# Down-projection of a gated decoder block: block products over pairs of tiles in place of the plain product

## The chip, the cores and the metric

The kernel runs on one core of a Trainium2 chip. The metric is the device time of one execution in microseconds (us), the median of several runs. The core has a matrix engine (TensorE, PE), a vector engine (VectorE, DVE), an activation engine (ScalarE, ACT), a general engine (GpSimd, POOL), and SyncE (SP), whose queue issues nearly all DMA transfers here. Each engine runs its own instructions in order and waits for the others on semaphores. SBUF holds 128 partitions; PSUM has 8 banks of 128x512 float32 numbers, which matrix products accumulate in.

## The reference, cut to what matters

```
def gdfn(h, w_up, dw_w, dw_b, w_down):
    u = jnp.einsum("bsd,df->bsf", h, w_up)
    u = causal_dwconv(u, dw_w, dw_b)
    a, g = jnp.split(u, 2, axis=-1)
    return jnp.einsum("bsf,fd->bsd", jax.nn.gelu(a) * g, w_down)
...
    x = x + jnp.einsum("bsd,de->bse", merged, mix_w_out[l])
    h = rmsnorm(x, norm_ffn[l])
    x = x + gdfn(h, ffn_w_up[l], ffn_dw_w[l], ffn_dw_b[l], ffn_w_down[l])
return rmsnorm(x, norm_final)
```

There is one sequence of 1024 positions, D_MODEL is 1024 and D_FF is 2816. Before this part the layer has a convolution branch and a pooling branch, which the change leaves alone. All data are float32.

## The kernel before, in words

Channels lie on the partitions and positions along the row, so x is 8 tiles of 128x1024, and the gated activations gelu(a)*g are 22 tiles. For accuracy each float32 operand of a product is split in two parts: the high part is a rounded copy that ACT writes (w_high, gated_high), the low part is the operand less its high part, written by POOL for weights (w_low) and by DVE for gated tiles (gated_low). Each product of 128x128 by 128x512 is then three matmuls (three, lines 1395 to 1399): high by low, low by high, high by high.

The up-projection runs over pairs p = 0 to 21 of an a tile and a g tile. From pair 2 on it uses a seven-product scheme over a 2x2 blocking (output tile of the pair, half of the input channels) by (half of the input channels, half of the positions): seven products of 12 matmuls (PRODUCTS, in the order P1, P6, P5, P7, P2, P4, P3) take the place of eight. DVE does the sums after the products (lines 1294 to 1323), then the convolution's taps (line 1254), ACT the gelu (line 875), and DVE multiplies (gate, line 1269). The product, a gated tile, goes to DRAM (keep_g, line 428), since SBUF still holds h and its sums. The operands of the scheme lie in h_hi, h_lo, cv_r and ga_r; a part of these comes free with each product of the last pair, and becomes the home of gated tiles.

The down-projection follows. The 22 gated tiles are loaded back (load_g, line 434), one at a time in two buffers of tmp, split by ACT and DVE and put into 14 homes (G_HOME). The down weights are 44 operands of 128x512: for turn 0 to 3 (half of the gated tiles, half of the output tiles) 11 operands each. They come in 11 blocks of four (1 MB; ffn_weights, line 424) into two buffers, and pass through a ring of 8 places. PE does 4 output tiles by 2 halves for each operand (down_tile), accumulates over 11 gated tiles in PSUM, and DVE adds the result to x (evict, line 1340). The last turn runs half by half and quarter by quarter of the positions, and the final norm runs beside and behind it (lines 1356 to 1375).

SP issues in the order in which its program is written: around the up stage's end it stores the last gated tiles, loads the first ones, and then alternates a block, three gated tiles and a piece of x (lines 424 to 465). A load waits there until its buffer is free; a load written behind it is issued after it.

## Time and profile before

| what | value |
|---|---|
| median of 3 runs | 1348.48 us (1346.82 to 1350.67) |
| profiled execution | 1348.21 us, its span 1346.4 us, mean granted clock 0.996 |
| busy share of the span | PE 99%, DVE 58%, ACT 29%, POOL 54% |
| matmuls | 6084 |
| DMA | 118.65 MB, mean 88 GB/s |

The span reaches from the first to the last instruction, so the rest of the execution's time lies around it. Busy shares are means over stages with different limits. The up-projection's pairs fill the time up to about 1092 us, the down-projection and the final norm the rest.

### The profile page before, as it was taken

Reading aid. Unit: us, or ns where it says so; the run is one execution under the profiler, and the core shown is the slowest. Engines: PE = TensorE matmul, PEld = TensorE weight load, DVE = VectorE, ACT = ScalarE, POOL = GpSimd, SP = SyncE. Lnnn points to the kernel's source line nnn. Section 1 sums busy time; section 2 is a strip of 40 time slices with the busy share of each in tenths; the row PEclk is TensorE's granted clock in tenths of the full one; section 3 lists DMA queues with packets and bytes.
Section 4 is the critical chain, followed back from the end, with each engine's and each line's share of the span. In section 5 each row is a group of like instructions: output and inputs, shape, how many; then the busy total and the mean of one; then the engine's idle time right before and its main releaser. Section 6 shows DMA issues by size and latency. Waiting matters only on the chain.

```text
span 1346.4 us, 15879 instructions
## 1 busy us (share of the span) xinstructions
PE 1328.3 (99%) x6084; PEld 1106.2 (82%) x6084; DVE 783.8 (58%) x919; ACT 395.6 (29%) x534; POOL 721.8 (54%) x477
## 2 busy tenths in 40 slices
PE   8999999999999999999998999999999999999997
PEld 7888888888887888878887888888888888788887
DVE  5898999999556255536595545554455543320224
ACT  5212121211114440011154444444344433322210
POOL 4536645553553343366858978777787714424101
PEclk9999999999999999999999999999999999999999
DMA  9201111111111113244313212222222238431003
GB/s 336 79 32 53 41 47 48 33 59 34 47 47 48 47 48 109 78 172 134 117 43 114 94 63 94 91 82 68 90 94 78 94 133 304 173 110 63 0 1 125
DMA packets 33025, 118.65 MB, mean 88 GB/s; under 512 B 3136, under 2 KB 7232, under 8 KB 28864
## 3 DMA queue, kind: packets, MB, share of 16 engines
q1 hardware_dynamic: 29280, 108.31, 22.8%
q10 hardware_dynamic: 3680, 9.44, 1.9%
q8 instruction: 45, 0.74, 0.2%
q14 instruction: 20, 0.16, 0.0%
HBM read 97.82 MB, written 19.92 MB: 87 GB/s over the span
## 4 chain that ended last, share of the span: by engine, by line
PE 87%; DVE 5%; DMA 3%; issue 1%; ACT 1%; POOL 1%; SPq 0%; POOLq 0%; DVEq 0%; ACTq 0%
PE ps L1397 29%; PE ps L1398 29%; PE ps L1399 29%; DMA tmp<-g_kept 2%; DVE ga_r L1248 1%; DVE tmp L1158 1%; DMA cv<-in_x 1%; DVE raw L1254 1%; DVE ga_r L1273 0%; PE ps L1461 0%; ACT cv L654 0%; PE ps L1451 0%; DVE res L1241 0%; DVE res L1239 0%; DVE res L1238 0%
## 5 line engine op out<-in xcount | busy, mean ns | idle before, releaser
L1397 PE MATMUL ps<-h_lo,w_hi 128*128 128x512 f32 (+1 forms) x924 | 357.9, 387 | 1.9 <-DVE h_lo L1016 1.9
L1399 PE MATMUL ps<-h_hi,w_hi 128*128 128x512 f32 (+1 forms) x924 | 356.0, 385 | 0.0
L1398 PE MATMUL ps<-h_hi,w_lo 128*128 128x512 f32 (+1 forms) x924 | 356.0, 385 | 0.0
L507 POOL TENSOR_SCALAR w_hi<-raw 128x1024 fp32r<-128x1024 f32 x62 | 68.5, 1105 | 290.1 <-issue 241.1
L1397 PEld LDWEIGHTS ps<-h_lo,w_hi 128*128 128x128 f32 x924 | 173.5, 188 | 38.1 <-DVE h_lo L1016 3.1
L1398 PEld LDWEIGHTS ps<-h_hi,w_lo 128*128 128x128 f32 x924 | 173.5, 188 | 34.9 <-issue 0.2
L1399 PEld LDWEIGHTS ps<-h_hi,w_hi 128*128 128x128 f32 x924 | 173.5, 188 | 34.8
L1397 PE MATMUL ps<-ga_r,w_hi 128*128 128x512 f32 (+1 forms) x428 | 166.1, 388 | 4.8 <-POOL w_lo L593 3.0
L1398 PE MATMUL ps<-cv_r,w_lo 128*128 128x512 f32 (+1 forms) x428 | 165.3, 386 | 0.0
L1399 PE MATMUL ps<-cv_r,w_hi 128*128 128x512 f32 (+1 forms) x428 | 165.3, 386 | 0.0
L1096 DVE SCALAR_TENSOR_TENSOR ps<-tmp,par,ps 128x512 f32<-128x512 f32 x224 | 158.4, 749 | 0.0
L509 POOL TENSOR_TENSOR w_lo<-raw,w_hi 128x1024 fp32r<-128x1024 f32 x62 | 154.1, 2486 | 5.2
L593 POOL TENSOR_TENSOR h_lo<-tmp,h_hi 128x512 fp32r<-128x512 f32 x66 | 94.1, 1439 | 61.1 <-ACT h_hi L885 60.8
L1397 PEld LDWEIGHTS ps<-ga_r,w_hi 128*128 128x128 f32 x428 | 80.8, 189 | 22.3 <-issue 3.4
L1397 PE MATMUL ps<-ga_r,h_hi 128*128 128x512 f32 (+1 forms) x260 | 98.3, 378 | 0.0
L1399 PE MATMUL ps<-cv_r,h_hi 128*128 128x512 f32 (+1 forms) x260 | 97.8, 376 | 0.0
L1398 PE MATMUL ps<-cv_r,h_lo 128*128 128x512 f32 (+1 forms) x260 | 97.8, 376 | 0.0
L1398 PEld LDWEIGHTS ps<-cv_r,w_lo 128*128 128x128 f32 x428 | 80.9, 189 | 16.0
L1399 PEld LDWEIGHTS ps<-cv_r,w_hi 128*128 128x128 f32 x428 | 80.7, 189 | 16.2
L593 POOL TENSOR_TENSOR w_lo<-tmp,w_hi 128x512 fp32r<-128x512 f32 x48 | 68.5, 1440 | 42.0 <-ACT w_hi L885 41.8
L1096 DVE SCALAR_TENSOR_TENSOR ps<-cv,both_w,ps 128x512 f32<-128x512 f32 x120 | 89.9, 749 | 0.0
L1397 PE MATMUL ps<-h_lo,h_hi 128*128 128x512 f32 (+1 forms) x232 | 87.8, 378 | 0.8 <-POOL w_lo L593 0.8
(197 smaller groups left out, 2030.2 us busy)
## 6 DMA issues: line engine op xcount, KB each, us to landing
raw<-in_wstream SPq DMA_DIRECT2D x68, 512.0 KB, 3.4
tmp<-in_wffn SPq DMA_DIRECT2D x16, 1024.0 KB, 4.8
tmp<-g_kept SPq DMA_DIRECT2D x22, 512.0 KB, 4.6
res<-in_wffn SPq DMA_DIRECT2D x10, 1024.0 KB, 4.8
g_kept<-res SPq DMA_DIRECT2D x14, 512.0 KB, 2.6
raw<-in_wffn SPq DMA_DIRECT2D x5, 1024.0 KB, 4.8
res<-in_xT ACTq DMA_DIRECT2D x4, 1024.0 KB, 4.8
x_kept<-res ACTq DMA_DIRECT2D x16, 256.0 KB, 2.3
```

Of the source, the lines that this page charges most:

```text
L507: pool.tensor_scalar(hi, r, 1.0, 0.0, ALU.mult, ALU.add).then_inc(w_hi_done, 1)
L509: pool.tensor_tensor(lo, r, hi.bitcast(f32), ALU.subtract).then_inc(w_split, 1)
L593: pool.tensor_tensor(lo, src, hi.bitcast(f32), ALU.subtract).then_inc(f_wlo, 1)
L1096: dve.scalar_tensor_tensor(out=out, in0=x, scalar=w, in1=acc, op0=ALU.mult, op1=ALU.add).then_inc(conv_tap, 1)
L1158: dve.tensor_tensor(csum, csum, sq[k % 2], ALU.add).then_inc(summed, 1)
L1248: dve.tensor_tensor(four(ga_r, at), src, four(cv_r, at).bitcast(f32), ALU.subtract).then_inc(t_lo, 1)
L1254: dve.scalar_tensor_tensor(out=acc[:, d:], in0=slot(s, 0, SEQ - d), scalar=par1("ffn_w", f * 3 + 2 - d), in1=acc[:, d:], op0=ALU.mult, op1 ...
L1397: nc.tensor.matmul(out, a_hi, b_lo, start=start, stop=False, skip_group_check=onto)
L1398: nc.tensor.matmul(out, a_lo, b_hi, start=False, stop=False, skip_group_check=onto)
L1399: return nc.tensor.matmul(out, a_hi, b_hi, start=False, stop=stop, skip_group_check=onto)
```

## The change

The down-projection takes the seven-product scheme too. Its 2x2 blocking is (even or odd output tile) by (even or odd gated tile) by (half of the positions). The seven products are D1, D6, D3, D5, D7, D2, D4; each is done for 4 pairs of output tiles (m) and over 11 pairs of gated tiles, which makes a group of 33 matmul positions, so 99 matmuls on the three parts. The names:

- A *piece* is a 128x512 operand on the gated side. There are seven kinds: a half of an even tile (B11), the halves of an odd tile (B21, B22), and four sums (T1 to T4), which DVE makes in the up stage for each two gated tiles (gated_sums). All seven are stored in DRAM (keep_even, keep_odd). A *unit* is two pieces (128x1024, 0.52 MB; the sixth of a product is a single one); each product needs six units, units 0 to 5 for D1, 6 to 11 for D6, 12 to 17 for D3 and so on, 42 in all. Twelve have a home at a time. They pass through two buffers: load_u, unit_high on ACT, unit_low on DVE.
- A *weight operand* d is for one product, one m and one chunk c of 4, 4 or 3 gated pairs (512, 512 or 384 columns), 84 in all; d0 to d11 are D1's, d12 to d35 alternate D6 and D3. They pass through the ring: down_high on ACT, down_low on POOL.
- A *block* is the raw weights as they are loaded (load_block): 0 to 3 for D1 (0.72 MB each), 4 to 15 for D6 and D3 together (1.05 MB, or 0.79 MB for a third chunk), 16 to 39 for D5 and D7, 40 to 47 for D2 and D4. Block 4 gives d12 and d13, block 5 d14 and d15. DVE sums quarters of it (weight_sums), for D3 POOL makes one more sum. Four places hold a large block each: a block waits until the low parts made from the one before it in its place are there (ops_before_block).

PSUM holds each group in one of 6 banks, and DVE adds or subtracts it into one to four halves of x (add_group). PE runs all of D1; then for each m D6 and D3 chunk by chunk in turn; then the others product by product. The last groups of D2 and D4 are done in quarters of the positions, first-half ones last, and the final norm's order changes with it.

```
+OPS = [(D1, m, c) for m in range(MP) for c in range(3)]
+OPS += [(q, m, c) for m in range(MP) for c in range(3) for q in (D6, D3)]
+OPS += [(q, m, c) for q in (D5, D7) for m in range(MP) for c in range(3)]
+OPS += [(q, m, c) for q in (D2, D4) for m in range(MP - 1) for c in range(3)]
+OPS += [(q, MP - 1, c) for q in (D2, D4) for c in range(3)]
+def block_place(b):
+    if b < FIRST_HALVES:
+        return (2 * (b % 4), 2 * (b % 4) + 1)
+    if b < LAST_HALVES:
+        return (b % 8,)
+    return (0, 1) if b % 2 == 0 else (6, 7)
+def ops_before_block(b):
+    users = [d for d in range(N_OPS) if block_of(d)[0] < b and set(block_place(block_of(d)[0])) & set(block_place(b))]
+    return max(users) + 1 if users else 0
+ADDED = {D1: ((0, 0, 0), (0, 1, 0), (1, 0, 1), (1, 1, 1)), D6: ((0, 1, 1), (1, 0, 0), (1, 1, 0)), D3: ((0, 1, 0),),
+         D5: ((0, 1, 0), (1, 1, 1)), D7: ((1, 0, 0), (1, 1, 0)), D2: ((0, 0, 0),), D4: ((1, 0, 0),)}
+UNITS_AFTER = {11: (8,), 13: (9, 10), 15: (11,), 17: (12, 13), 18: (14, 15), 19: (16, 17), 38: (18, 19), 40: (20, 21),
...
+LOADS = ("b4 b5 b6 u8 u9 b7 b8 u10 u11 b9 u12 b10 u13 u14 u15 b11 u16 u17 b12 u18 u19 b13 b14 b15 b16 b17 b18 b19 b20 b21 "
...
+            def keep_odd(i):
+                sp.wait_ge(f_g, 2 * i + 2)
+                wait(sp, o_kept[i % 2], 48 * (i // 2))
+                sp.dma_start(g_d[:, 1:3, i, :], two_pieces(acc_b[(2 * i + 1) % 3])).then_inc(o_kept[i % 2], 16)
+                sp.wait_ge(g_t, 4 * i + 4)
+                sp.dma_start(g_d[:, 3:5, i, :], two_pieces(acc_a[2 * i % 3])).then_inc(o_kept[i % 2], 16)
+                sp.dma_start(g_d[:, 5:7, i, :], two_pieces(acc_a[(2 * i + 1) % 3])).then_inc(o_kept[i % 2], 16)
+            def load_u(u):
...
+                if u >= 2:
+                    sp.wait_ge(g_lo, u - 1)
+                sp.dma_start(u_raw(u), g_d[:, o, i:i + n, :]).then_inc(g_back[u % 2], 16)
+            def load_block(b):
+                q, m, c = BLOCKS[b]
+                wait(sp, f_wlo, FIRST_DOWN + ops_before_block(b))
...
+            for u in range(2, UNITS):
+                load_u(u)
+            sp.wait_ge(f_used, operand(FT - 1, P4) + 1)
+            load_block(1)
+            load_block(2)
+            load_x1(0)
+            sp.wait_ge(o_kept[(FP - 2) % 2], 48 * ((FP - 2) // 2 + 1))
+            load_x1(1)
+            load_u(UNITS)
+            load_u(UNITS + 1)
+            keep_odd(FP - 1)
+            sp.wait_ge(o_kept[(FP - 1) % 2], 48 * ((FP - 1) // 2 + 1))
+            load_block(3)
+            load_x1(2)
             sp.wait_ge(f_post, posted(FT - 1, "c12"))
...
+            load_x1(3)
+            for what in LOADS:
...
-            for d in range(N_DOWN):
-                b = FT - PLAIN + d // 4
-                if d % 4 == 0:
-                    pool.wait_ge(f_raw[b % 2], 16 * (b // 2 + 1))
-                w_low(FIRST_DOWN + d, quarter(raw_down[b % 2], d % 4))
+            for d, (q, m, c) in enumerate(OPS):
+                b = block_of(d)[0]
+                if q == D3:
+                    pool.wait_ge(d_sum, sums_of(b))
+                    pool.tensor_tensor(quarter_of(b, 1), quarter_of(b, 0), quarter_of(b, 1), ALU.add).then_inc(d_sum4, 1)
+                down_low(d)
...
+            def highs(d0, d1):
+                for d in range(d0, d1):
+                    down_high(d)
+                    for u in UNITS_AFTER.get(d, ()):
+                        unit_high(u)
...
+            def gated_sums(i):
+                e, o, t12, t34 = acc_b[2 * i % 3], acc_b[(2 * i + 1) % 3], acc_a[2 * i % 3], acc_a[(2 * i + 1) % 3]
+                (e1, e2), (o1, o2), (t1, t2), (t3, t4) = ((t[:, 0:HALF], t[:, HALF:SEQ]) for t in (e, o, t12, t34))
+                dve.wait_ge(f_g, 2 * i + 2)
+                dve.tensor_tensor(t1, e1, e2, ALU.subtract).then_inc(g_t, 1)
+                dve.tensor_tensor(t3, e2, o2, ALU.subtract).then_inc(g_t, 1)
+                dve.wait_ge(g_t, 4 * i + 1)
+                dve.tensor_tensor(t2, t1, o2, ALU.add).then_inc(g_t, 1)
+                dve.wait_ge(g_t, 4 * i + 3)
+                dve.tensor_tensor(t4, o1, t2, ALU.subtract).then_inc(g_t, 1)
...
+            def weight_sums(b0, b1):
+                for b in range(b0, b1):
+                    dve.wait_ge(d_raw[block_place(b)[0]], 16 * block_count(b))
+                    if BLOCKS[b][0] == D6:
+                        w11, w12, w21, w22 = (quarter_of(b, i) for i in range(4))
+                        dve.tensor_tensor(w21, w21, w22, ALU.add).then_inc(d_sum, 1)
+                        dve.wait_ge(d_sum, sums_of(b) - 1)
+                        dve.tensor_tensor(w11, w21, w11, ALU.add).then_inc(d_sum, 1)
+                    else:
+                        dve.tensor_tensor(quarter_of(b, 0), quarter_of(b, 0), quarter_of(b, 1), ALU.add).then_inc(d_sum, 1)
...
+            def chunk(d, out, a=0, b=HALF):
+                q, m, c = OPS[d]
+                pe.wait_ge(f_wlo, FIRST_DOWN + d + 1)
+                for i in range(4 * c, 4 * c + CHUNKS[c]):
+                    u = UNITS * q + i // 2
+                    if m == 0 and i % 2 == 0:
+                        pe.wait_ge(g_lo, u + 1)
+                    a_hi, a_lo = ring_tile(FIRST_DOWN + d, i - 4 * c)
+                    mm = three(out, a_hi, a_lo, u_piece(h_hi, cv_r, u, i % 2)[:, a:b], u_piece(h_lo, ga_r, u, i % 2)[:, a:b],
+                               i == 0, i == FP - 1)
```

Three engines' orders at the place that the prediction speaks of follow. SP first, from the store of the last gated tile on; L424 is a block, L434 a gated tile and L465 a piece of x. Before:

```order
L428 DMA g_kept<-raw 128x1024 [waits f_g]
L424 DMA raw<-in_wffn 128x2048 [waits f_wlo,g_kept0]
L434 DMA tmp<-g_kept 128x1024 [waits g_lo,g_kept1]
L434 DMA tmp<-g_kept 128x1024 [waits g_lo,g_kept2]
L424 DMA tmp<-in_wffn 128x2048 [waits f_post,f_wlo,g_kept1,g_kept2]
L434 DMA tmp<-g_kept 128x1024 [waits g_lo,g_kept0]
L465 DMA res<-x_kept 128x4x1024
```

SP in the changed kernel, the same place; L548 to L551 store the odd tile's pieces and sums, L572 is a block, L561 a unit, L575 a piece of x:

```order
L548 DMA g_kept<-raw 128x2x512 [waits o_kept0,f_g]
L550 DMA g_kept<-res 128x2x512 [waits g_t]
L551 DMA g_kept<-raw 128x2x512
L572 DMA raw<-in_wffn 128x1408 [waits f_wlo,o_kept0]
L575 DMA res<-x_kept 128x2x1024
L575 DMA res<-x_kept 128x2x1024 [waits f_post]
L572 DMA tmp<-in_wffn 128x2048 [waits f_wlo]
L572 DMA cv<-in_wffn 128x2048 [waits f_wlo]
L572 DMA ga<-in_wffn 128x4x384 [waits f_wlo]
L561 DMA tmp<-g_kept 128x2x512 [waits g_lo,o_kept1,o_kept0] x2
L572 DMA raw<-in_wffn 128x2048 [waits f_wlo]
L572 DMA tmp<-in_wffn 128x2048 [waits f_wlo]
```

Ahead of the down stage's second set of operands there now stand three stores, the wait for their end (o_kept0), a block, two pieces of x, and three more blocks; unit 10 comes behind the last row.

ACT, where the high parts of weight operands (L885) and gated tiles (L909) take turns, before:

```order
L885 ACTIVATE w_hi<-raw 128x512 [waits f_used,f_raw1]
L909 ACTIVATE cv_r<-tmp 128x1024 [waits f_used,g_back0]
L885 ACTIVATE w_hi<-raw 128x512 [waits f_used]
L909 ACTIVATE cv_r<-tmp 128x1024 [waits f_used,g_back1]
L885 ACTIVATE w_hi<-raw 128x512 [waits f_used]
```

ACT in the changed kernel, from d9 (the first row) to d15 and unit 11; L1064 is a weight operand, L1074 a unit:

```order
L1064 ACTIVATE h_hi<-raw 128x512 [waits f_used,d_raw6]
L1064 ACTIVATE h_hi<-raw 128x512 [waits f_used]
L1064 ACTIVATE h_hi<-raw 128x384 [waits f_used]
L1074 ACTIVATE h_hi<-tmp 128x2x512 [waits f_used,g_back0]
L1064 ACTIVATE w_hi<-tmp 128x512 [waits f_used,d_sum]
L1064 ACTIVATE w_hi<-tmp 128x512 [waits f_used,d_sum4]
L1074 ACTIVATE h_hi<-tmp 128x2x512 [waits f_used,g_back1]
L1074 ACTIVATE h_hi<-tmp 128x2x512 [waits f_used,g_back0]
L1064 ACTIVATE w_hi<-cv 128x512 [waits f_used,d_sum]
L1064 ACTIVATE w_hi<-cv 128x512 [waits f_used,d_sum4]
L1074 ACTIVATE h_hi<-tmp 128x512 [waits f_used,g_back1]
```

Unit 8 now stands ahead of d12, units 9 and 10 ahead of d14, and d13 and d15 wait for a sum that POOL makes (d_sum4).

DVE in the changed kernel after the last gated sums; L1473 is a unit's low part, L1541 and L1543 are a block's sums, L1557 adds a group into x. Before, the low parts of ten tiles (L1273) followed one another here.

```order
L1473 TENSOR_TENSOR ga_r<-tmp,cv_r 128x1024 [waits g_hi] x2
L1541 TENSOR_TENSOR tmp<-tmp 128x512 [waits d_raw0]
L1543 TENSOR_TENSOR tmp<-tmp 128x512 [waits d_sum]
L1541 TENSOR_TENSOR cv<-cv 128x512 [waits d_raw2]
L1543 TENSOR_TENSOR cv<-cv 128x512 [waits d_sum]
L1541 TENSOR_TENSOR ga<-ga 128x384 [waits d_raw4]
L1543 TENSOR_TENSOR ga<-ga 128x384 [waits d_sum]
L1473 TENSOR_TENSOR h_lo<-tmp,h_hi 128x2x512 [waits g_hi]
L1557 TENSOR_TENSOR res<-res,ps 128x512 [waits x1_back0,f_used]
```

The sums of three blocks stand between the low parts of units 7 and 8.

## Rows read from the trace of the kernel before

**Rows 1.** The page, section 1: busy us, share, instructions of each engine.

```profile
PE 1328.3 (99%) x6084; PEld 1106.2 (82%) x6084; DVE 783.8 (58%) x919; ACT 395.6 (29%) x534; POOL 721.8 (54%) x477
```

**Rows 2.** PE's waits from 1050 us to the end: us in total, times, longest.

```profile
PE ps L1451 <- DVE tmp L1369: 1.5, 1, 1.5
PE ps L1397 <- POOL w_lo L593: 0.8, 1, 0.8
```

**Rows 3.** Stretch of the down stage: us, busy of PE, PEld, DVE, ACT, POOL, clock, DMA, GB/s.

```profile
1110.00:1130.00 20.00, 20.00 (x90) 16.57 (x89) 7.66 (x5) 7.84 (x11) 10.30 (x6) 1.00 0.91 335
```

**Rows 4.** Timeline of PE: start us, us, engine, line, operation.

```profile
849.92 0.39 PE L1399 MATMUL ps<-cv_r,w_hi 128*128 128x512 f32 x1
...
882.57 0.39 PE L1399 MATMUL ps<-h_hi 128*128 128x512 f32 x1
...
1334.04 0.28 PE L1399 MATMUL ps<-h_hi 128*128 128x256 f32 x1
...
1336.56 0.28 PE L1399 MATMUL ps<-cv_r,w_hi 128*128 128x256 f32 x1
```

**Rows 5.** Timeline of ACT.

```profile
1123.80 1.06 ACT L909 ACTIVATE cv_r<-tmp 128x1024 fp32r<-128x1024 f32 x1 [7.01 <-DMA tmp<-g_kept]
...
1240.06 0.63 ACT L885 ACTIVATE h_hi<-tmp 128x512 fp32r<-128x512 f32 x1 [4.87 <-PE ps L1399]
```

**Rows 6.** Timeline of POOL.

```profile
1138.58 1.82 POOL L593 TENSOR_TENSOR h_lo<-tmp,h_hi 128x512 fp32r<-128x512 f32 x1 [5.60 <-ACT h_hi L885]
1140.36 2.26 POOL L593 TENSOR_TENSOR w_lo<-raw,w_hi 128x512 fp32r<-128x512 f32 x1
...
1213.51 1.29 POOL L593 TENSOR_TENSOR w_lo<-raw,w_hi 128x512 fp32r<-128x512 f32 x1 [4.02 <-ACT w_hi L885]
```

**Rows 7.** Timeline of DVE, with the idle time before and its releaser.

```profile
1069.99 0.70 DVE L1320 TENSOR_TENSOR ps<-ps,res 128x512 f32<-128x512 f32 x1 [4.02 <-PE ps L1399]
...
1091.75 0.70 DVE L1323 TENSOR_TENSOR ps<-res,ps 128x512 f32<-128x512 f32 x1 [2.02 <-PE ps L1399]
...
1099.72 1.23 DVE L1269 TENSOR_TENSOR raw<-raw 128x1024 f32<-128x1024 f32 x1
...
1138.01 1.23 DVE L1273 TENSOR_TENSOR ga_r<-tmp,cv_r 128x1024 fp32r<-128x1024 f32 x1 [6.18 <-ACT cv_r L909]
1139.49 2.00 DVE L1273 TENSOR_TENSOR ga_r<-tmp,cv_r 128x1024 fp32r<-128x1024 f32 x1 [0.25 <-ACT cv_r L909]
...
1288.99 0.69 DVE L1369 TENSOR_TENSOR tmp<-tmp 128x512 f32<-128x512 f32 x1 [0.70 <-ACT tmp L994]
```

**Rows 8.** Landing: chain of work from 900 us, tile g_kept, DMA issues (KB each, median us).

```profile
1114.30 9.47 DMA tmp<-g_kept
...
DMA to landing us min/median/max: 2.6/3.2/9.5
...
tmp<-in_wffn SPq DMA_DIRECT2D x16, 1024.0 KB, 4.8
```

**Rows 9.** Timeline of SP's queue, issues only.

```profile
1103.62 0.33 SPq L424 DMA_DIRECT2D raw<-in_wffn  x1
1104.05 0.85 SPq L434 DMA_DIRECT2D tmp<-g_kept  x2
1105.08 0.63 SPq L424 DMA_DIRECT2D tmp<-in_wffn  x1
1112.07 0.32 SPq L434 DMA_DIRECT2D tmp<-g_kept  x1
1112.44 0.43 SPq L465 DMA_DIRECT2D res<-x_kept  x1
```

**Rows 10.** Clock and warm-up: last stretch of the windows; PE's first matmuls.

```profile
1342.00:1346.40 4.40, 0.00 (x0) 0.00 (x0) 0.67 (x2) 0.00 (x0) 0.76 (x2) 0.50 0.71 238
...
1.84 5.22 PE L1478 MATMUL ps<-ident,ones 128*128 128x128 f32 x28 [1.84 <-POOL ident L499]
...
8.43 2.84 PE L1478 MATMUL ps<-ident,ones 128*128 128x128 f32 x24
```

597 lines of the change are left out of this document (363 added, 234 removed).

## The prediction

> **What bounds the kernel now.** I read the page's first section, then the stretches of the down stage, PE's waits there, and the timelines of PE, DVE, POOL, ACT and SP around its start. PE is busy 99% of the span [rows 1]; in the stretch from 1050 us to the end it waited for DVE 1.5 us and for POOL 0.8 us [rows 2]. So PE's own work sets the time, and every matmul taken away is worth its spacing. The stage is less comfortable for the others: at 1110 to 1130 us the DMA engines are busy 91% at 335 GB/s, while PE is never idle [rows 3].
>
> **What goes (PE).** 512-column matmuls start 0.2267 us apart (144 from 849.92 to 882.57 [rows 4]), 256-column ones 0.120 us apart (21 from 1334.04 to 1336.56 [rows 4]). Before, the down stage has 22 x 8 x 2 x 3 = 1056 of full width, the last quarter's second half cut in two: 924 x 0.2267 + 264 x 0.120 = 241.2 us. After, 7 x 4 x 11 x 3 = 924, of which the last two groups (66) are cut in two: 858 x 0.2267 + 132 x 0.120 = 210.4 us. Gain: 30.8 us, if nothing starves. The norm's tail is the same chain of 256-column steps in both (last product at 1336.56, end 1346.4) and I cost its change at 0, within 1 us either way.
>
> **What comes on the other engines.** Per operation: ACT's high part 0.63 us for 128x512, 1.06 for 128x1024 [rows 5]; POOL's low part 1.29 [rows 6]; DVE 1.23 for 128x1024, 0.69 for 128x512 [rows 7]. Counts: weight operands 44 -> 84 (a third of them 384 wide, by proportion 0.97 on POOL), 12 D3 sums on POOL, 48 weight sums on DVE, 42 unit lows (35 of 1.23, 7 of 0.69) for 22, 44 gated sums.
> The gated sums (4 x 0.69 = 2.8 us per two pairs) stand in the up stage between the readers of P7 and of P4. There DVE sits idle 4.0 us for PE (line 1320 at 1069.99 [rows 7]), so they cost 0. In turns with POOL (4 x 1.29 us more, see below) they would be 4 us late every second pair, and PE needs that sum only two pairs later. Bounds 0 and 5 us.
> The loads grow too. Blocks: 44 x 0.26 MB = 11.5 MB become 31.7 MB; gated pieces: 11.5 MB become 20.2 MB each way.
>
> **The start of the down stage, step by step.** P3 of the last pair ends at 1091.7 (DVE's last post sum starts at 1091.75 [rows 7]). D1 is 4 x 33 x 0.2267 = 29.9 us, so D6 should start at 1121.6. Its first operands come late, because of what SP's queue holds ahead of them:
> 1. gate(21) ends at 1100.95 in the trace [rows 7]. Now ACT and DVE also serve units 2 to 5 before it: unit 4's load must wait for the low of unit 2, so it lands near 1093, its high and low run to 1095.2, and taps and gate(21) end near 1103. The gated sums end near 1106; the last stores then take 2.6 us or more (the fastest of g_kept's transfers is 2.6 [rows 8]), say 1110. SP waits for them (their buffers are block 3's place) and only then issues block 3, two x1 pieces, blocks 4, 5, 6, units 8 and 9.
> 2. Does the queue serve these one after the other? The g_kept load issued at 1114.30 landed 9.47 us later, against a median of 3.2 [rows 8, 9]; ahead of it were a 1 MB block, unit loads and 2 MB of x1. From 1103.62 on 6.3 MB were issued and the last landed at 1123.8: 342 GB/s after taking off 1.8 us of fixed time (3.2 us less 0.52 MB's transfer). 335 GB/s at a share of 0.91 is 368 when full [rows 3]. I take 360 GB/s, in order of issue.
> 3. Block 3 (0.72 MB) lands at 1114; high and low to 1116; D1's fourth group (due 1114.3) waits **1.8 us**.
> 4. Unit 8 has 6.2 MB up to its own end: 17.3 + 1.8 us, lands 1129.4. ACT takes unit_high(8) before down_high(12), though block 4 landed at 1123. High of unit 8 to 1130.5, of d12 to 1131.1, its low (behind DVE's unit low) 1133.0. PE was due at 1123.4: **9.6 us**.
> 5. D3's first operand (d13) is summed and split after that: 1.3 + 0.6 + 1.3 = 1136.2. Only then may SP issue block 8, and only behind it unit 10: (1.05 + 0.52)/0.36 + 1.8, lands 1142.6. ACT waits for it in order; then d14, the sum, d15: 1150. Only then block 9 and, behind it, unit 12: 1155.8; high, low: 1158.1. PE finished D6's first chunk at 1135.7 and needs unit 12 for D3's: **22.5 us**.
> 6. Unit 13 stands behind block 10: 1162.5 for 1159.6, **2.9**; units 14, 15: **0.3**; unit 16 stands behind block 11, which waits for d19's low: **6.0**.
> Sum of the waits: 43.1 us. Wrong by at most: from below, all loads land as if alone (3.2 us, and 4.8 for a block [rows 8]). Then d12 is ready at 1119.8, d13 at 1123.1, unit 10 lands at 1126.7, d15 ends at 1132.9, unit 12's low at 1138.8 against 1124.6: 14.2, and 2.3 + 3.4 for the later ones, 20 us in all. From above, 335 GB/s and every POOL step behind a DVE one add some 10: 53 us.
>
> **The rest of the stage.** POOL does per pair of D6 and D3 operands low, sum, low: 3.9 us, and 0.7 for ACT's high between, against 5.44 us of PE. From D3 to D5 the units' homes are used again at once: unit 20 is issued only after the low of d38, unit 22 after the low of unit 20; worked as above they come 1 to 2 us late. The later products have a whole product (29.9 us) between the release of a home and its use. Cost 3 us; bounds 0 and 15.
> Here a row speaks against the change. DVE's low alone took 1.23 us at 1138.01, but 2.00 at 1139.49 while POOL worked on 1138.58 and 1140.36, which took 1.82 and 2.26 in place of 1.29 [rows 6, 7]: they take turns. In turns, the D6/D3 stretch needs on POOL 12 x 3 x 1.29 = 46.4 us, less 12 x 0.32 for the 384-wide ones: 42.6; on DVE 24 sums (15.5) and 12 unit lows (13.7): 72 us for 59.8 us of PE, of which a lead of the ring and DVE's work before it take a part. The Trainium skill (SBUF — State Buffer, "SBUF: two separate sides") says that the port pair which DVE and GpSimd share is locked for a whole instruction, the other one fully blocked, when the DVE operation has two SBUF inputs. By that rule, the trace agrees (2.00 for 1.23), and sums into PSUM stay free. It is the port rival below.
> PE's clock: in the last 4.4 us, after the products ended, the granted clock is 0.50, the 1.2 GHz level [rows 10]. At the kernel's start 28 matmuls took 5.22 us where 24 later ones took 2.84, so 28 would have taken 3.3: coming out of idleness costs up to 1.9 us. After waits of 9.6 and 22.5 us the first matmuls run so, but D6's first chunk is followed by a wait that hides it. Cost 1 us; bounds 0 and 6.
>
> **Sum.** The profiled execution took 1348.21 us (span 1346.4 and 1.8 around it), 0.3 under the median of 1348.48. 1348.2 - 30.8 + 43.1 + 3 + 1 = 1364.5, so 1364 us.
>
> **Rivals.**
> - *Transfers land beside each other* (faster). The order of the queues still costs 20 us, the rest 0 to 5: 1337 to 1343, 1340 us. For it: most transfers landed in 3.2 us. Against: 9.47 us at 1114.30, and more bytes now. It decides where block 4 lands before 1117.
> - *The lead hides nearly all* (faster): the ACT and SP order is late nowhere by more than the ring holds: 1348.2 - 30.8 + 5 = 1322. Against: unit 12 cannot be issued before d15's low, and that needs block 4, issued after 1110.
> - *The shared port binds* (slower): the D6/D3 stretch takes 72 us, the D5 and D7 stretch (POOL 28, DVE 43) also goes over PE's in places: 12 to 18 us on top of 43: 1376 to 1382, 1379 us. Decides where DVE's operations with two SBUF inputs and POOL's together exceed 59.8 us in a stretch of that length. Against: much of DVE's share falls into the waits that are there anyway.
> - *The gain and the waits cancel* (no change): waits of 27 to 35 us in all, part of the transfers beside each other: 1348.
>
> **Chances.** My forecast 0.53 (own range 1353 to 1375), beside each other 0.22, hidden 0.08, port 0.08, cancel 0.09. What a measurement can tell from no change is 0.3% (4 us). Faster: 0.22 + 0.08 and 0.01 of the last = 0.31; same 0.08; slower 0.53 + 0.08 = 0.61. The range leaves out the hidden case and most of the port's: 1336 to 1377.
>
> **What would show it.** Matmuls of 128x512 in the down stage 858, and PE's waits there 40 to 50 us, nearly all between 1114 and 1180: one near 9 us ahead of D6's first matmul with POOL's low as releaser, one above 15 us ahead of D3's with DVE's unit low. On SP's queue, block 8 issued within 1 us of d13's low, near 1136. POOL and DVE idle in between. DMA busy above 0.85 from 1110 to 1134 and low after it. It is wrong if block 4's sum starts before 1118, if unit 12 is issued before 1145, or if PE's waits after 1180 exceed 15 us.

## The result and the profile after

| | before | changed |
|---|---|---|
| median, lowest and highest of the runs | 1348.88 us (1346.82 to 1350.67) | 1411.53 us (1408.17 to 1413.25) |
| profiled execution | 1348.21 us, span 1346.4 | 1408.17 us, span 1406.3 |
| mean granted clock | 0.996 | 0.968 |

The ratio is 1.0462, 95% interval [1.0437, 1.0487]: 63 us slower. Forecast were 1364 us and slower; the direction is right, the size is off by 47 us in the median (44 us in the profiled execution, for which the sum was made) and outside the range (1336 to 1377).

The page of the changed kernel, section 1 (busy us, share, instructions), answers to [rows 1]. PE is busy 8 us less with 198 matmuls fewer, DVE 146 us more, POOL 75 us more. (A group is 33 matmuls, 11 pairs by three parts; the 99 in the section on the change is wrong, the prediction counts with 33.)

```profile
PE 1320.2 (94%) x5886; PEld 1091.1 (78%) x5886; DVE 929.6 (66%) x1066; ACT 431.4 (31%) x596; POOL 796.6 (57%) x529
```

PE's waits from 1050 us on (us in total, times, longest) answer to [rows 2]. Before they were 2.9 us in all: the two rows there and one of 0.6 us for DVE that they leave out. Now they are 68.7:

```profile
PE ps L1670 <- DVE h_lo L1473: 26.7, 5, 20.3
PE ps L1724 <- DVE cv L1605: 15.5, 1, 15.5
PE ps L1670 <- POOL w_lo L743: 10.1, 3, 6.3
PE ps L1670 <- POOL h_lo L743: 6.2, 2, 3.2
PE ps L1670 <- DVE ga_r L1473: 4.8, 1, 4.8
PE ps L1670 <- DVE res L1498: 1.8, 1, 1.8
PE ps L1724 <- DVE cv L1623: 1.5, 1, 1.5
PE ps L1670 <- DVE res L1494: 1.5, 1, 1.5
PE ps L1734 <- DVE small L1194: 0.6, 1, 0.6
```

PE's timeline shows where the longest stand (start, us, the wait in brackets). In this order: one of 2.43 us in the up stage, then the waits ahead of D1's fourth group, of D6's first chunk, of D3's first (unit 12) and of D3's third (unit 16), two in D7, and the one ahead of the final variance.

```profile
740.26 0.50 PE L1670 MATMUL ps<-ga_r,w_hi 128*128 128x512 f32 x1 [2.43 <-DVE res L1494]
...
1125.28 0.76 PE L1670 MATMUL ps<-h_lo,h_hi 128*128 128x512 f32 x1 [3.16 <-POOL h_lo L743]
1142.19 0.77 PE L1670 MATMUL ps<-ga_r,w_hi 128*128 128x512 f32 x1 [6.33 <-POOL w_lo L743]
1166.85 0.76 PE L1670 MATMUL ps<-h_lo,w_hi 128*128 128x512 f32 x1 [20.35 <-DVE h_lo L1473]
1187.51 0.77 PE L1670 MATMUL ps<-ga_r,h_hi 128*128 128x512 f32 x1 [4.79 <-DVE ga_r L1473]
1280.97 0.50 PE L1670 MATMUL ps<-ga_r,h_hi 128*128 128x512 f32 x1 [3.01 <-POOL h_lo L743]
1299.21 0.79 PE L1670 MATMUL ps<-ga_r,w_hi 128*128 128x512 f32 x1 [3.50 <-POOL w_lo L743]
1337.62 1.87 PE L1724 MATMUL ps<-mean_w,cv 128*128 128x1 f32 x8 [15.52 <-DVE cv L1605]
```

Stretches of the changed kernel (columns as in [rows 3]). The first is that of [rows 3]: PE 16.84 of 20 us where it was never idle, DMA share about the same. In the second and third the clock is 0.50, the 1.2 GHz level. In the last PE is busy throughout.

```profile
1110.00:1130.00 20.00, 16.84 (x65) 13.49 (x64) 6.79 (x7) 3.69 (x5) 5.55 (x5) 0.86 0.85 313
1140.00:1144.00 4.00, 1.81 (x4) 1.50 (x5) 3.19 (x5) 0.86 (x3) 3.12 (x3) 0.50 0.03 12
1164.00:1172.00 8.00, 3.14 (x7) 2.07 (x8) 3.90 (x5) 3.57 (x4) 0.96 (x1) 0.50 0.68 255
1200.00:1240.00 40.00, 39.88 (x176) 32.67 (x175) 28.82 (x30) 11.57 (x19) 29.09 (x21) 1.00 0.70 231
```

**The account of 60.0 us** (1408.2 - 1348.2): matmuls that went -30.8; waits 68.7 + 2.4 (up stage) less the 2.9 + 0.8 of before, +67.4; the rest, 23.4 us, is matmuls at the slow clock (0.427 us apart for 0.227). The waits are 2.4 in the up stage, 3.3 in the last pair, 36.6 from D1 to D3 (3.16 + 6.33 + 20.35 + 2.01 + 4.79), 4.3 in D5, 6.8 in D7, 15.5 at the final variance, and 2.1 behind it as before.

### The profile page after: what moved, and what is told of

Its sections match the earlier page's. It is cut to its first block, busy times and chain, and to the rows that moved or that the text cites. A ratio compares the mean times of both kernels' runs of the same rounds, so it can differ in the third digit from the quotient of the medians.

```text
span 1406.3 us, 15940 instructions
## 1 busy us (share of the span) xinstructions
PE 1320.2 (94%) x5886; PEld 1091.1 (78%) x5886; DVE 929.6 (66%) x1066; ACT 431.4 (31%) x596; POOL 796.6 (57%) x529
## 3 DMA queue, kind: packets, MB, share of 16 engines
HBM read 126.65 MB, written 28.57 MB: 110 GB/s over the span
## 4 chain that ended last, share of the span: by engine, by line
PE 72%; DMA 8%; DVE 7%; POOL 6%; ACT 3%; issue 2%; SPq 1%; DVEq 0%; ACTq 0%; POOLq 0%
PE ps L1670 24%; PE ps L1672 24%; PE ps L1671 24%; DMA tmp<-g_kept 7%; POOL h_lo L743 2%; POOL w_lo L743 2%; DVE ga_r L1435 1%; DVE tmp L1345 1%; DVE raw L1441 1%; DMA cv<-in_x 1%; ACT w_hi L1064 1%; DVE h_lo L1473 0%; PE ps L1734 0%; PE ps L1724 0%; DMA tmp<-in_wffn 0%
## 5 line engine op out<-in xcount | busy, mean ns | idle before, releaser
L1670 PE MATMUL ps<-h_lo,w_hi 128*128 128x512 f32 (+1 forms) x969 | 376.8, 389 | 28.9 <-DVE h_lo L1473 26.7
L1671 PE MATMUL ps<-h_hi,w_lo 128*128 128x512 f32 (+1 forms) x969 | 374.1, 386 | 0.0
L1672 PE MATMUL ps<-h_hi,w_hi 128*128 128x512 f32 (+1 forms) x969 | 373.9, 386 | 0.0
L1670 PEld LDWEIGHTS ps<-h_lo,w_hi 128*128 128x128 f32 x969 | 182.9, 189 | 69.6 <-issue 26.0
L1672 PEld LDWEIGHTS ps<-h_hi,w_hi 128*128 128x128 f32 x969 | 182.9, 189 | 36.6
L1671 PEld LDWEIGHTS ps<-h_hi,w_lo 128*128 128x128 f32 x969 | 182.9, 189 | 36.5 <-issue 0.2
L1670 PE MATMUL ps<-ga_r,w_hi 128*128 128x512 f32 (+1 forms) x386 | 154.3, 400 | 19.5 <-POOL w_lo L743 9.8
L1671 PE MATMUL ps<-cv_r,w_lo 128*128 128x512 f32 (+1 forms) x386 | 153.0, 396 | 0.0
L1672 PE MATMUL ps<-cv_r,w_hi 128*128 128x512 f32 (+1 forms) x386 | 152.8, 396 | 0.0
L1671 PE MATMUL ps<-h_hi,h_lo 128*128 128x512 f32 (+1 forms) x214 | 82.9, 388 | 0.0
```

Of the source, the lines that this page charges most:

```text
L1670: nc.tensor.matmul(out, a_hi, b_lo, start=start, stop=False, skip_group_check=onto)
L1671: nc.tensor.matmul(out, a_lo, b_hi, start=False, stop=False, skip_group_check=onto)
L1672: return nc.tensor.matmul(out, a_hi, b_hi, start=False, stop=stop, skip_group_check=onto)
```

## Experiments

The kernels start from the changed one unless said otherwise. A and B are the theories of the expectation that stands ahead of each result. For a comparison that the up stage does not blur, the table splits each profiled span at DVE's last post sum of the last pair but one (Q), the same instruction in all kernels: 1072.71 before, 1075.16 in the changed kernel.

```profile
1075.16 0.70 DVE L1526 TENSOR_TENSOR ps<-res,ps 128x512 f32<-128x512 f32 x1 [0.87 <-PE ps L1672]
```

Each of the last two columns is one execution. e12 and e13 have the same code behind Q and differ by 4.4 us there, so a few us in the last column prove nothing alone. The kernel before, run beside each of them, took 1347.9 to 1349.2 us. e7 and e11 leave sums out, so their products get wrong operands; the others calculate what the changed kernel does.

| kernel | median us | ratio to before, 95% | Q | Q to the end |
|---|---|---|---|---|
| before | 1348.9 | | 1072.7 | 273.7 |
| changed | 1411.5 | 1.0462 [1.0437, 1.0487] | 1075.2 | 331.1 |
| e1 block 0 | 1408.9 | 1.0444 [1.0427, 1.0462] | 1079.1 | 328.1 |
| e2 fillers, too long | 1426.0 | 1.0569 [1.0552, 1.0587] | 1079.6 | 347.1 |
| e3 units first | 1402.3 | 1.0395 [1.0378, 1.0412] | 1077.0 | 324.3 |
| e4 norm first | 1399.2 | 1.0370 [1.0353, 1.0387] | 1079.6 | 321.5 |
| e5 fillers | 1412.6 | 1.0477 [1.0459, 1.0494] | 1079.0 | 331.3 |
| e6 x1 late | 1407.8 | 1.0443 [1.0425, 1.0460] | 1076.9 | 327.3 |
| e7 gated sums on one column | 1405.7 | 1.0419 [1.0395, 1.0444] | 1072.3 | 330.8 |
| e8 orders | 1388.2 | 1.0290 [1.0269, 1.0312] | 1078.0 | 308.3 |
| e9 and places | 1359.9 | 1.0094 [1.0077, 1.0110] | 1076.7 | 280.3 |
| e10 fillers at the end | 1410.1 | 1.0465 [1.0447, 1.0482] | 1076.8 | 328.9 |
| e11 weight sums on one column | 1404.4 | 1.0416 [1.0399, 1.0434] | 1079.0 | 325.2 |
| e12 e9 and five moves | 1360.1 | 1.0086 [1.0072, 1.0101] | 1081.2 | 277.9 |
| e13 gated sums back | 1361.4 | 1.0093 [1.0078, 1.0107] | 1075.5 | 282.3 |
| e14 variance later | 1353.2 | 1.0024 [1.0011, 1.0037] | 1080.1 | 272.2 |
| e15 D5's units ahead | 1355.0 | 1.0051 [1.0037, 1.0065] | 1076.8 | 276.0 |
| e16 D6's and D3's too | 1353.7 | 1.0041 [1.0027, 1.0055] | 1079.0 | 274.8 |
| e17 lows of 20 and 21 ahead | 1348.2 | 0.9997 [0.9987, 1.0006] | 1079.6 | 268.0 |
| e18 gated sums divided | 1345.9 | 0.9984 [0.9974, 0.9994] | 1075.3 | 268.2 |

**e1: block 0.**

```diff
-            def load_block(b):
+            def load_block(b, first=False):
...
-                wait(sp, f_wlo, FIRST_DOWN + ops_before_block(b))
+                if not first:
+                    wait(sp, f_wlo, FIRST_DOWN + ops_before_block(b))
...
-            load_block(0)
+            load_block(0, first=True)
```

> Block 0's load no longer waits for the lows of the last pair (its place is free two pairs earlier); nothing else is changed. Theory A (the load of block 0, issued only at 1077.6, and with it the load of unit 0 and the last gated stores behind it on SP, delays ACT's first down operand by 5.7 us and through ACT's order the copy of pa and P7, P4 and P3 of the last pair): the last pair ends about 5 us earlier, at 1094 to 1096 in place of 1099.7, block 3 is issued about as much earlier, and the kernel takes 5 to 8 us less, 1403 to 1407 us. Theory B (the last pair is late because of the four new unit loads, each of which has to wait for the low of the one before the last): nothing moves, 1409 to 1412 us.

Measured 1408.9 us, 2.7 less, and 3.0 less from Q to the end; the intervals of the two kernels overlap, and the time lies between the ranges of A and B. The last pair ends 19.3 us after Q in place of 24.6. So the cause of the pair's late end is A's. The gain behind it is smaller: the last gated stores wait for gate(21), which ends 32.3 us after Q in place of 36.1, and D6 starts 3.9 us earlier (63.1 after Q for 67.0).

**e2: matmuls on constants in the waits.**

```diff
+            WARM = {9: 22, 12: 48, 13: 160, 17: 36, 50: 22, 55: 26}   # by operand, and 125 ahead of final_variance(0)
...
+                    nc.tensor.matmul(bank(7, 0, P), ones[:, :], ident[:, :], start=True, stop=True)
```

> Matmuls on constants (128x128, into a bank nobody reads, about 0.11 us each) fill the seven long waits of PE in the down stage: 22 ahead of D1's fourth group, 48 ahead of D6, 160 ahead of D3, 36 ahead of unit 16's chunk, 22 and 26 in D7, 125 ahead of the final variance. Each series is a bit shorter than its wait. Nothing else is changed. Theory A (the time of the slow clock after the waits is paid in full, 18.7 us in the changed kernel, of which some 15 stand behind these waits): granted clock 0.95 or more from 1124 to 1200 and after 1337, and the kernel takes 10 to 16 us less, 1396 to 1402 us. Theory B (a slow stretch only shortens the wait that follows it, since the operands come from ACT, DVE and POOL at a pace that PE's clock does not set): 0 to 5 us less, 1407 to 1411 us, and longer waits in place of the slow matmuls. Between the two: the clock's cost is paid where no wait follows, that is behind unit 16 and behind the final variance, 5 to 10 us.

A miss of mine: 439 such matmuls left 878 records of 0.11 us, two each, and went on past the waits: 1426.0 us, 14.5 us slower, clock 0.993. It says only how long they take and decides nothing between A and B.

**e5: half as many** (11, 24, 80, 18, 11, 13, 62).

> The same filling matmuls as in the earlier run, but half as many: each of them takes two passes of 0.11 us, so that in the earlier run they went on long past the waits (it had no wait left ahead of D6 and D3 and was 15 us slower than the changed kernel). Now 11, 24, 80, 18, 11, 13 and 62, or 2.5, 5.4, 18.0, 4.1, 2.5, 2.9 and 14.0 us, each a bit shorter than its wait. Theory A (the slow clock after the waits is paid in full): granted clock 0.99 over the span and 10 to 15 us less than the changed kernel, 1396 to 1402 us. Theory B (a slow stretch only shortens the next wait, because the operands come at a pace that PE's clock does not set): 0 to 5 us less, 1406 to 1411 us, the waits behind the fillers grown by about what the slow matmuls took before.

1412.6 us, no different from the changed kernel's 1411.5 within the measurement, with a clock of 0.990 for 0.968. Its waits from 1050 us on are 31.6 us (the longest rows below), and 49.3 us of filling matmuls (219 of 0.225) stand where the rest was:

```profile
PE ps L1670 <- DVE h_lo L1473: 12.3, 5, 3.7
PE ps L1670 <- POOL w_lo L743: 5.8, 3, 3.5
PE ps L1724 <- DVE cv L1605: 3.0, 1, 3.0
PE ps L1670 <- DVE ga_r L1473: 2.6, 3, 0.9
```

Theory B: D3's start comes 92.1 us after Q (91.7 in the changed kernel), unit 16's 113.1 (112.3), the final variance 262.3 (262.5), though from 1050 us on the matmuls lost only 9.6 us to their full rate, in the changed kernel 22.2. Waits and fillers together are 80.9 us for 68.7: they grew by 12.2 us, what the slow matmuls gave back. From D1 to the variance other engines set the pace; a slow matmul there only shortens the next wait.

**e10: fillers only ahead of the final variance** (74; the wait that e5 left there, 3.0 us, had let the clock fall again).

> Filling matmuls only ahead of the final variance, 74 of 0.225 us = 16.7 us, about the whole of that wait; everything else is as in the changed kernel. Behind this wait stand 33 matmuls of D2 and then D4 with operands long ready, so the slow clock of 5 us should be paid here if anywhere. Theory A (paid in full where no wait follows): from the variance to the last instruction 66.0 to 66.5 us in place of 68.7, granted clock 1.00 behind it, and about 2.5 us less than the changed kernel, 1408 to 1410 us. Theory B (something else paces the tail): 68.5 us or more again, 1411 to 1413 us.

1410.1 us, 1.4 less, which the intervals cannot tell from nothing; the stretch itself is clearer. PE's timeline behind the variance, first the changed kernel's (0.77 us for the first matmul, at 1.2 GHz), then e10's from its variance on:

```profile
1339.35 0.77 PE L1670 MATMUL ps<-ga_r,w_hi 128*128 128x512 f32 x1
```

```profile
1339.51 1.05 PE L1724 MATMUL ps<-mean_w,cv 128*128 128x1 f32 x8 [0.81 <-DVE cv L1605]
1340.42 0.49 PE L1670 MATMUL ps<-ga_r,w_hi 128*128 128x512 f32 x1
```

From there to the end it takes 66.2 us in place of 68.7 (69.0 in e5, where the clock was low too): A. Here, with operands long ready, the slow clock is paid, 2.5 us.

**e3: units ahead of blocks on SP's list** (the part of LOADS that changes).

```diff
-u8 u9 b7 b8 u10 u11 b9 u12 b10
+u8 u9 b7 u10 u11 u12 b8 b9 u13 b10
```

> On SP's list of loads units 10 and 11 go ahead of block 8 and unit 12 ahead of blocks 8 and 9; nothing else is changed. Theory A (the order of SP's queue makes D3's start late: block 8 waits for the low of d13, block 9 for that of d15, and the units behind them wait too): unit 10 is issued near 1140 in place of 1145.7, the wait ahead of D3 falls from 20.4 to 6 to 10 us, and the kernel takes 8 to 14 us less, 1397 to 1403 us. Theory B (the wait goes over to the next on the list: DVE takes the sums of blocks 7 to 9 ahead of unit 12's low, and block 9 still comes late): the wait ahead of D3 falls by less than 5 us, 1406 to 1410 us.

1402.3 us, 9.3 less; D3's wait is 13.4 us in place of 20.4. The time is A's, with a longer rest of the wait than I had put (6 to 10). Why the rest is longer no run shows; units 10 to 12 still go through the two small buffers one after another, and DVE's sums stand ahead of unit 12's low.

**e6: x1's last two pieces behind unit 9.**

> The last two of the four loads of x1 (2 MB in all) go behind unit 9 on SP's list, in place of ahead of block 4; nothing else is changed. Theory A (the queue's transfers share 360 GB/s in order of issue): blocks 4 to 6 and unit 8 land some 5 us earlier, unit 8's high starts at 1133 in place of 1138.5, the wait ahead of D6 falls from 6.3 to 0 to 2 us; what that brings D3's start is less, since block 8 and unit 10 still stand behind d13's low: the kernel takes 4 to 7 us less, 1404 to 1407 us. Theory B (the transfers run beside each other, and unit 8 lands late for another reason): unit 8's high stays within 1 us of 1138, 1410 to 1412 us.

1407.8 us. Unit 8's high on ACT, in the changed kernel and in e6:

```profile
1138.49 1.06 ACT L1074 ACTIVATE h_hi<-tmp 128x1024 fp32r<-128x1024 f32 x1 [13.76 <-DMA tmp<-g_kept]
```

```profile
1135.13 1.06 ACT L1074 ACTIVATE h_hi<-tmp 128x1024 fp32r<-128x1024 f32 x1 [8.25 <-DMA tmp<-g_kept]
```

That is 63.3 us after Q and 58.2: 5.1 us earlier for 2 MB less ahead of it. D6's wait falls from 6.3 to 1.0 us. In the changed kernel the first sums of blocks 4, 5 and 6, issued at 1120.15, 1120.82 and 1121.47, start as each of them lands:

```profile
1131.07 0.69 DVE L1541 TENSOR_TENSOR tmp<-tmp 128x512 f32<-128x512 f32 x1 [14.22 <-DMA tmp<-in_wffn]
1135.07 0.69 DVE L1541 TENSOR_TENSOR cv<-cv 128x512 f32<-128x512 f32 x1 [2.58 <-DMA cv<-in_wffn]
1137.17 0.56 DVE L1541 TENSOR_TENSOR ga<-ga 128x384 f32<-128x384 f32 x1 [0.68 <-DMA ga<-in_wffn]
```

From block 3's issue at 1118.77 to unit 8's landing 6.2 MB took 19.7 us, 348 GB/s after the prediction's 1.8 us of fixed time. So the transfers do share the rate in about the order of issue (A); the rival of transfers beside each other, which wanted block 4 before 1117, is out.

**e4: norm ahead of the last units.**

```diff
-               65: (36, 37), 66: (38, 39), 67: (40, 41)}
+               65: (36, 37)}      # highs of 38 to 41 now behind the squares
...
-            unit_low(*range(36, 42))
+            unit_low(36, 37)       # lows of 38 to 41 behind the half sums
             groups(D7, 3)
```

> The norm goes ahead of the last units: ACT takes the squares of the finished half before the highs of units 38 to 41, DVE the additions of D7's fourth group and the half sums before their lows. Nothing else is changed. Theory A (the 15.5 us that PE waits for the final variance are the squares' place in ACT's order behind four units that are loaded one after the other): PE's wait ahead of the final variance falls below 3 us, the slow clock after it goes too, and the kernel takes 12 to 17 us less, 1394 to 1399 us. Theory B (units 38 to 41 then come late for D4's first group and the wait only moves there): less than 5 us, 1406 to 1411 us, with a wait of 8 us or more ahead of D4.

1399.2 us, 12.4 less, the variance's wait 3.2 us, and no wait ahead of D4: A. (From Q to the end its profile has 9.6 us less; that execution, 1403.0 us, was the longest of four.)

**e7: the gated sums on one column.**

> The four sums over a pair of gated tiles are made on one column in place of 512, so DVE does next to nothing for them (the products that use them get wrong operands); stores and loads are as in the changed kernel. Theory A (the sums cost PE nothing but one wait of 2.4 us at 740 and their part of the last pair's end, where they stand ahead of the last stores): 3 to 6 us less, 1405 to 1409 us. Theory B (in turns with POOL's weight sums they lengthen DVE's path in all pairs and the last pair): 10 us less or more, 1401 us or under. Theory C (hidden altogether): 1410 to 1412 us.

1405.7 us, 5.8 less, all of it ahead of Q (330.8 us behind it, 331.1 in the changed kernel). Of the wait at 740 us 0.66 is left. So the sums cost some 6 us, in one place. DVE's timeline of the changed kernel in the first pair of the seven-product scheme shows it: the four take 6.9 us in turns with POOL, and the post sum at L1523 starts at 733.73.

```profile
727.05 1.67 DVE L1463 TENSOR_TENSOR raw<-raw 128x512 f32<-128x512 f32 x1
728.64 1.77 DVE L1464 TENSOR_TENSOR res<-raw,res 128x512 f32<-128x512 f32 x1
730.34 1.77 DVE L1466 TENSOR_TENSOR raw<-raw,res 128x512 f32<-128x512 f32 x1
732.14 1.67 DVE L1468 TENSOR_TENSOR res<-res,raw 128x512 f32<-128x512 f32 x1
733.73 0.69 DVE L1523 TENSOR_TENSOR ps<-ps,res 128x512 f32<-128x512 f32 x1
```

In the kernel before it started at 727.34, and DVE had 0.65 us of room there; the 4.0 us of [rows 7] are those of a late pair.

```profile
727.34 0.69 DVE L1320 TENSOR_TENSOR ps<-ps,res 128x512 f32<-128x512 f32 x1
728.67 0.69 DVE L1323 TENSOR_TENSOR ps<-res,ps 128x512 f32<-128x512 f32 x1 [0.65 <-PE ps L1399]
```

**e11: DVE's weight sums on one column.**

> DVE's sums of weight blocks (48 operations of 128x512 with two operands in SBUF, ahead of D6, D3, D5 and D7) are made on one column in place of 512; the products get wrong operands, all loads, highs, lows and POOL's sums stay. Theory A (the order of loads and of ACT bounds the stage, DVE and the port that it shares with POOL do not): 2 to 5 us less, from the steps that stand on the path to D6, D3 and D5's start (a sum of 1.3 to 2 us each ahead of d12, d14, d16), 1406.5 to 1409.5 us; between the wait for unit 16 and D5's start nothing changes. Theory B (the port rival: DVE's and POOL's turns bind): 10 us less or more, 1401 us or under, and POOL's 128x512 operations near 1.29 us throughout.

1404.4 us, 7.1 less: between the two. The last 190 matmuls ahead of unit 20, where the changed kernel has its first wait in D5, take 43.1 us in both kernels, the full rate of 0.2267 us each. So the port does not bind the rest of D6 and D3. D3's start comes 92.1 us after Q for 91.7, so the sums do not set it either. The gain is there at the start of D5: PE begins on unit 22 167.2 us after Q for 172.3, with one wait (1.4 us) in place of three (4.3), and the first wait of D7 ends at 200.8 for 205.8. The sums stand ahead of unit lows there, and I had placed their price ahead of D6.

**e8: orders together.** e1, e4, ACT's and DVE's orders at the same place (left out here), and

```diff
             load_block(2)
+            load_block(4)
             load_x1(0)
...
+            load_block(5)
             keep_odd(FP - 1)
...
-b4 b5 b6 u8 u9 b7 b8 u10 u11 b9 u12 b10 u13
+u8 b6 u9 u10 x2 u11 b7 u12 x3 b8 b9 u13 b10
```

> The orders are changed together: block 0 without its wait, the norm ahead of the last units, blocks 4 and 5 issued as soon as their places are free (ahead of the last gated stores), x1's last two pieces behind units 10 and 12, units 8 to 12 ahead of blocks 6 to 9 on SP's list, and on ACT and DVE units 8, 12 and 13 each where its load has landed. No calculation is changed. If the waits of D1 to D3 are the orders' alone (theory A), the waits ahead of D1's fourth group, D6 and D3 come to 12 us or less in place of 30, and the time is 2.7 and 12.4 us (the two parts run alone) and some 20 to 24 us under 1411.5: 1372 to 1377 us. If the transfers themselves bound this stretch (theory B: 15 MB from 1110 to 1140 at 360 GB/s are 42 us), the waits stay at 20 us or more in sum and it is 1383 to 1390 us.

1388.2 us. The waits from D1's fourth group to unit 17 are 30.2 us (7.8 + 6.5 + 5.5 + 6.6 + 3.8), and the time is in B's range, so by my numbers it was B, the transfers. The next run shows that it was not.

**e9: e8 with other places and a later D3.**

```diff
-        return (2 * (b % 4), 2 * (b % 4) + 1)
+        at = (0, 3, 1, 2)[(b - 3) % 4]      # from block 3 on
+        return (2 * at, 2 * at + 1)
...
-OPS += [(q, m, c) for m in range(MP) for c in range(3) for q in (D6, D3)]
+OPS += [(q, 0, c) for q in (D6, D3) for c in range(3)]
+OPS += [(q, m, c) for m in range(1, MP) for c in range(3) for q in (D6, D3)]
```

> All of the earlier run with changed orders, and in addition: block 3 goes to the place that block 0 leaves (free some 25 us before the gated tiles' place that it had to wait for), block 4 takes the gated tiles' place; in the first group D6 runs its three chunks before D3's, so that D3's units are due 7.5 us later; units 13 to 17 and 20 to 29 stand further ahead on SP's list, and units 24 to 35 further back in ACT's order. No calculation is changed. Theory A (what is left of the waits is still order): the wait ahead of D1's fourth group (7.8 us there) goes, the waits from D6's start to unit 17 fall from 22 to 5 to 10 us, those of D5 and D7 from 12 to 6 us, and the time from 1388 to 1360 to 1368 us. Theory B (the transfers bound the stretch): the waits up to unit 17 stay at 20 us or more in sum, 1376 to 1384 us, with the DMA engines' share near 1 in most of 1110 to 1160.

1359.9 us, 28 less. The waits from D6's start to unit 17 are 11.9 us, D1's fourth group has none, nor has D7; D5 has 4.2 us and the variance 5.5. The time is A's. That is all order and place: both kernels read 126.65 MB and write 28.57 MB. Which of the moves (the places, the later D3, the lists of SP, ACT and DVE) brings how much is not separated.

**e12: five more moves** (block 4 in a free place, squares and half sums group by group, the first gated sums one pair later, lows of units 10, 11, 18, 19 ahead of sums).

> From the last run with changed orders and places (1359.9 us) on, with no change to what is calculated: blocks 4 and 5 take places that are free before the last gated stores have landed, so that D6's start no longer waits for these (4.3 us there); units 10 and 11's lows go ahead of block 6's sums; D5's first two units' lows ahead of four of its blocks' sums (3.1 us there); the first pair's gated sums stand one pair later (2.4 to 5.4 us in the up stage); the norm's squares and half sums are made as the groups finish, not all behind the last (5.5 us there, and 2.4 us of slow clock behind it). If the waits are all order (theory A), 11 to 15 us go and the time is 1345 to 1349 us, level with the kernel before. If the round trip of the units (load, high, low, next load: 5.5 to 6 us for two) bounds D3's start (theory B), D6's start comes on time but D3's waits grow by 2 to 4 us: 1348 to 1352 us. If an order that I moved stands in the way of another, 1352 us or more.

1360.1 us, no gain. That is the third case of the expectation, 1352 us or more: an order that I moved stands in another's way. The gated sums one pair later cost a wait of 4.2 us there (Q at 1081.2), and the 2.4 us less behind Q are within what one profile cannot tell.

**e13: e12 with these sums back in their place.**

> The last kernel (1360.1 us) with the first pair's gated sums back in their place, ahead of the last two post sums of the first pair; the rest of its orders stays. Theory A (the shift cost time: PE waited 4.2 us in the up stage for the u2 sum of a later pair and reached the end of the last pair but one at 1081.3, 4.5 us later than the run before it): that point comes at 1076 to 1078.5 and the time is 1355 to 1358 us. Theory B (the up stage loses the same wherever the sums stand, and the difference is that of one execution): 1359 to 1361 us.

1361.4 us, the same as e12: B. Q came earlier (1075.5), the rest took longer; one profile cannot tell a few us of these waits.

**e14: e13 with the final variance one group later.**

```diff
             group(D2, 0)
-            final_variance(0)
             group(D2, 1)
+            final_variance(0)
```

> As e13, and the final variance and its broadcast come one group of D2 later on PE (with DVE's addition of that group ahead of the inversion). In the last kernel PE waited 2.4 us for the variance's operand and 1.8 us for the inverted value, with a slow clock of some 5 us behind the first. Theory A (these are order): both waits are under 0.7 us and the time is 3 to 5 us below e13's. Theory B (the outputs of the first half, 8 operations on DVE behind the broadcast, then come late for the end): the same time as e13 or more, with a longer wait at the last broadcasts.

1353.2 us, 8.2 less: A, and more than the 3 to 5 forecast. The two waits were 5.5 us in e13 and are 0.7 now, and the matmuls behind the first take 2.0 us less over their full rate; the last us or so is not shown.

**e15: e14 with D5's units ahead of four blocks on SP's list; e16: also D6's and D3's units ahead of x1 and blocks.**

> As e14 (1353.2 us), with units 20 and 21 issued on SP ahead of blocks 23 and 24, units 22 and 23 ahead of block 26 (in e14 unit 20 was issued at 1207.1 behind seven blocks of D5 and landed 7.7 us later, and D5 waited 5.1 us for it). Theory A (the list's order): unit 20 lands within 4.5 us of its issue, D5's wait falls below 1.5 us and the time by 3 to 5 us, 1348 to 1350 us. Theory B (the homes of these units come free too late for any order): D5's wait stays at 3 us or more, 1351 to 1354 us.

> As e15, and x1's last two pieces go behind unit 17 on SP's list, units 13 to 17 ahead of the blocks that follow them, and DVE's additions of D1's third and fourth group behind the lows of units 12 to 17. Theory A (order and transfers): the five waits from D6's start to unit 17 (10 us in sum in e14) fall to 4 to 6 us and the time to 1343 to 1347 us, below the kernel before. Theory B (the round trip of two units, 5.5 to 6 us, is what is left): they stay at 8 us or more in sum and the time is that of e15 within 1.5 us.

1355.0 and 1353.7 us, no gain: B in both. D5's wait stayed (6.2 and 5.7 us): unit 20 lands 129.5 us after Q in e15 for 134.7 in e14, but DVE takes its low behind sums of blocks that now come later:

```profile
1210.48 0.69 DVE L1564 TENSOR_TENSOR tmp<-tmp 128x512 f32<-128x512 f32 x1 [3.69 <-DMA tmp<-in_wffn]
1212.62 3.15 DVE L1492 TENSOR_TENSOR h_lo<-tmp,h_hi 128x1024 fp32r<-128x1024 f32 x2
```

**e17: e16 with DVE's lows of units 20 and 21 ahead of these sums; e18: also the first pair's gated sums divided over two pairs.**

> As e16 (1353.7 us), with DVE's lows of units 20 and 21 ahead of the sums of blocks 22 to 24. Theory A (DVE's order held D5 up): D5's wait falls from 5.7 us to under 2, and the time by 3 to 5 us, 1348.5 to 1351 us, level with the kernel before. Theory B (the round trip): units 22 and 23 come late instead, 3 us or more of waits stay in D5, 1352 to 1354.5 us.

> As e17, with the first pair's four gated sums divided: two where they stood, two one pair later. Theory A (the first pair leaves DVE some 2 to 4 us of room in each of the two places, and all four together, 6.9 us in turns with POOL, are too long for either): the wait in the up stage falls to 0 to 2 us and the time to 1.5 to 4 us under e17's. Theory B (DVE is behind throughout the first pairs, whatever the place): the same time as e17 within 1 us.

1348.2 us, level with the kernel before, and 1345.9 us, faster than it by 0.06 to 0.26%, which is less than the 0.3% that the prediction takes as no change. In e17 the time is A's and the wait is B's: unit 20's wait is gone, and one of 4.1 us stands at unit 22, whose load SP issues at 1208.54, behind unit 20's low, and which lands at 1215.47. PE begins on unit 22 138.4 us after Q for 142.7 in e16, so most of the 5.5 us is won up to there. In e18 the wait in the up stage is 0.2 us (another of 1.8 stands later) and D5's, at unit 22 again, is 3.7. Its longest waits from 1050 us on:

```profile
PE ps L1711 <- DVE ga_r L1494: 7.2, 2, 4.2
PE ps L1711 <- DVE h_lo L1494: 6.6, 4, 3.7
PE ps L1711 <- POOL w_lo L752: 2.7, 1, 2.7
PE ps L1765 <- DVE cv L1663: 1.5, 1, 1.5
```

## Why the prediction was right in kind and wrong in size

**Right: the chain through SP's queue at the stage's start.** Counted from Q, forecast and measured: D6's start 60.3 and 67.0 us, block 8 issued 63.5 and 70.1, D3's start 85.4 and 91.7, the end of unit 16's wait 104.8 and 112.3. The shape holds, 6.3 to 7.5 us late throughout. (Steps 4 and 5 are 0.2 to 0.4 us off in their own sums, which changes nothing.) On SP's queue of the changed kernel block 8 is issued as the low of d13 ends (1145.18) and unit 10 behind it; block 9 and unit 12 likewise, behind the low of d15 (1158.24):

```profile
1145.21 0.34 SPq L572 DMA_DIRECT2D tmp<-in_wffn  x1
1145.67 1.00 SPq L561 DMA_DIRECT2D tmp<-g_kept  x2
1158.26 0.56 SPq L572 DMA_DIRECT2D cv<-in_wffn  x1
1158.93 0.56 SPq L561 DMA_DIRECT2D tmp<-g_kept  x1
```

The waits there are 36.6 us for 43.1, because PE itself came late: at D6 it was ready 60.7 us after Q for 50.7, the operand 67.0 for 60.3. The 342 to 368 GB/s in order of issue stood its test (e6).

**Missed: the last pair (step 1).** I took P3's end from the trace of before. Block 0's load waits for the lows of the last pair, which I had in the code and did not follow; unit 0 and the last gated stores but one stand behind it on SP, and ACT's first down operand ahead of the copy that DVE needs for u2:

```profile
1084.03 0.69 DVE L1494 TENSOR_TENSOR res<-res,ps 128x512 f32<-128x512 f32 x1 [4.48 <-ACT res L1111]
```

The pair ends 24.6 us after Q for 19.0, gate(21) ends 36.1 us after it for 30.3, and block 3 is issued at 1118.77 for my 1110, 43.6 us after Q for 37.3. This is the 6 to 7 us above. e1 takes block 3's issue back to 39.9 us after Q; what holds the remaining 2.6 us no run shows.

**Failed: the norm, costed at 0, within 1 us (paragraph on what goes).** I looked at the chain behind the last product and not at what stands ahead of the final variance. There PE has only one group of D2, 33 matmuls or 7.5 us, between D7's last product and the variance. ACT's eight squares stand behind the highs of units 38 to 41, which wait for their loads, and only then come one after the other with DVE's seven half sums (L1605), 7 us in all:

```profile
1321.82 1.06 ACT L1074 ACTIVATE cv_r<-tmp 128x1024 fp32r<-128x1024 f32 x1 [7.02 <-DMA tmp<-g_kept]
1327.94 1.57 ACT L1074 ACTIVATE cv_r<-tmp 128x1024 fp32r<-128x1024 f32 x2 [3.28 <-DMA tmp<-g_kept]
1330.94 1.65 ACT L1150 ACTIVATE cv<-res 128x512 f32<-128x512 f32 x3
```

```profile
1332.11 5.47 DVE L1605 TENSOR_TENSOR cv<-cv 128x512 f32<-128x512 f32 x7
```

It is 15.5 us of wait and 2.5 of slow clock (e4 gives back 12.4 us, e10 2.5), the largest single term of the miss.

**Mis-sized: the rest of the stage, 3 us (bounds 0 and 15).** D5 and D7 wait 11.1 us. The bound held, the value did not. In D7 (6.8 us) I had not counted that a high waiting for its unit's load holds ACT, which eats the ring's lead of 8 operands: PE waits for POOL's low of a weight operand at 1280.97, and ACT, ahead of that operand's high, had waited for a unit:

```profile
1275.27 1.06 ACT L1074 ACTIVATE cv_r<-tmp 128x1024 fp32r<-128x1024 f32 x1 [5.83 <-DMA tmp<-g_kept]
```

e9, by order alone, has no wait in D7. In D5 (4.3 us) order changes little: 4.2 us in e9, 4.1 and 3.7 in e17 and e18, there for unit 22, whose load waits for unit 20's low. I had put 1 to 2 us on it.

**Mis-sized: the gated sums, 0 (bounds 0 and 5).** 2.4 to 5.4 us of wait, 5.8 us with what follows (e7), above the bound: the row was read in a pair with room, the first pair has none; e18 divides them and 2.3 us come back (1348.2 to 1345.9, though the intervals of the two overlap).

**The clock, 1 us (bounds 0 and 6).** The slow matmuls are 23.4 us of PE's account, and yet the term is nearly right: only the 2.5 us at the end are shown to be paid, and e5 finds 0 from D1 to the variance. The Trainium skill (TensorE: Matmul & The Clock Gate, "HAM oscillation — how this bites in real kernels") counts half of the time at the lower clock as extra wall time. By that rule, with the granted clocks of the two kernels, e5 should have gained about 31 us (an estimate: 0.032 of 1406.3 us less 0.010 of 1410.3). It gained none, and the measurement decides for this kernel, whose operands come at other engines' pace.

**Sum of the miss**, 43.7 us (1408.2 less 1364.5): up to Q 2.4, the chain's late start 6.7 (D6's start); from there to D5's first chunk, 151.7 us after Q forecast and 161.9 measured (worked back from D5's first wait by the matmuls ahead of it), 3.5 more; from it to the end of the variance's wait 100.5 us for 70.3, which is 30.2 (15.5 norm, 8.1 waits of D5 and D7 over my 3, and 6.6 that the matmuls between the waits took over their full rate); tail 0.9.

**The rivals.** Transfers beside each other: out (e6). Lead hides all, and gain and waits cancel: out, with 68.7 us of waits. The shared port: operations do take turns (the rows of 1.67 to 1.77 us above for 0.69 alone), but PE was busy 39.88 of 40 us from 1200 to 1240, and e11 leaves that stretch as it was: not binding there. In D5 e11 takes the length of the sums away and their turns with POOL at once, so it cannot tell the two apart. Of the signs of being wrong, two did not come (block 4's sum started at 1131.07, unit 12 was issued behind 1158) and one did: PE's waits after 1180, put under 15 us, are 4.8 + 4.3 + 6.8 + 15.5 = 31.4.

**Is the change itself bad?** No, but it wins next to nothing: with the same products, sums and bytes as the changed kernel, e18 takes 268.2 us from Q to the end where the kernel before takes 273.7, and 1345.9 us for 1348.6 beside it. Of the 30.8 us of matmuls the rest goes into 19 us of waits and the slow clock behind them. What stays open: how much of these is the round trip of a unit through the two small buffers (no kernel with a third was tried), and how much of e14 to e17 is order against scatter.

## What to carry to other kernels

When operands go through a queue with a place to come free first, follow each wait that the new code adds on the issuing engine, the first of them included, and look for slack in the pair or group where the operation really stands, not in a steady one. When a product becomes shorter, look at what was timed against its length (a norm, a last load) and cost that at the bound, not at zero. Before a slower rewrite is given up, try the order of the loads, the places and the engine that holds a wait at the head of its line: here they were worth 65 us together, more than twice the 30.8 us of matmuls that the change takes away.

## What the runs showed of the hardware that was not expected

- Matmuls of 128x128 on plain 32-bit constants left two records of 0.11 us each, 0.225 us for one, back to back (e2: 878 records for 439; 99.2 us).
- The length of a wait alone does not tell whether the clock falls. In e5 the granted clock was 0.50 in the 4 us behind a wait of 3.00 us (ahead of the variance) and 1.00 behind one of 3.24 us (at 1246.62, in D5); in e10 it was 1.00 behind one of 0.81 us.
- Identical code up to Q reached it at 1075.2 to 1080.1 us in sixteen profiles (the changed kernel, e1 to e6, e8 to e11, e13 to e17), and the wait at 740 us was 2.4 in one and 5.4 in another; the kernel before has 0.8 there.
